# A ninth slot for the expert weights, and SBUF addresses at multiples of 128 bytes

## What is computed

```python
# first block
hx = modulate(rms_norm(x, norm_mix), sh1, sc1)
x = x + g1 * token_mix(hx, ...)           # h @ w_in, gated linear attention, conv, @ w_out
hx2 = modulate(rms_norm(x, norm_ffn), sh2, sc2)
aff = softmax(hx2 @ w_router)             # 512 x 16 experts
gate, idx = top_k(aff.T, 64)              # each expert takes 64 tokens
hid = silu(xs @ w_gate[e]) * (xs @ w_up[e])   # 1024 -> 2048, for 16 experts
x = x + g2 * scatter_add(idx, (hid @ w_down[e]) * gate)
# second block: rmsnorm, w_in, sparse attention, conv branch, merge,
# gated FFN with a convolution, a last gated projection, final rmsnorm
```

## Time and profile before

| | |
|---|---|
| median of 3 executions | 2129.46 us (2128.78 to 2130.61) |
| profiled execution | 2130.91 us, its span 2129.2 us |
| PE matmul busy | 2012.9 us, 95% |
| VectorE, ScalarE busy | 908.8 us (43%), 576.0 us (27%) |
| moved by DMA | 529.58 MB |

### The profile page before, as it was taken

One profiled execution on the slowest core, in us unless ns is written; L12 is line 12 of the kernel. 1 busy time (PEld: TensorE's weight loads), 2 busy tenths in 40 slices (PEclk: granted clock), 3 DMA queues, 4 the chain that ended last, 5 costly groups with the idle time before them and its releaser, 6 DMA issues.

```text
span 2129.2 us, 23757 instructions
## 1 busy us (share of the span) xinstructions
PE 2012.9 (95%) x9886; PEld 1264.0 (59%) x9886; DVE 908.8 (43%) x1489; ACT 576.0 (27%) x899; POOL 58.8 (3%) x107
## 2 busy tenths in 40 slices
PE   6999999899899999988899888999999999999998
PEld 4888777443343424242433323776688888888886
DVE  4666574311021111110101110877897656666545
ACT  5434323100010000000000000527725344344445
POOL 1000000000000000000000000005300000000000
PEclk9999999799999999999999999999999999999999
DMA  9462116699999999999999999151132332323222
GB/s 345 158 229 87 41 41 277 246 384 415 428 428 427 427 428 428 428 428 428 428 428 427 428 428 411 55 141 41 40 119 80 108 100 79 119 79 109 80 98 81
DMA packets 107931, 529.58 MB, mean 249 GB/s; under 512 B 15045, under 2 KB 43825, under 8 KB 82993
## 3 DMA queue, kind: packets, MB, share of 16 engines
q1 hardware_dynamic: 107825, 528.07, 62.0%
HBM read 525.95 MB, written 2.10 MB: 248 GB/s over the span
## 4 chain that ended last, share of the span: by engine, by line
PE 87%; DMA 7%; DVE 3%; issue 2%; ACT 1%; SPq 0%; ACTq 0%; DVEq 0%
PE bank L1033 21%; PE bank L624 14%; PE bank L625 14%; PE bank L626 14%; PE bank L1098 7%; DMA f<-in_w_gate_dram 4%; PE bank L990 3%; PE bank L1007 3%; PE bank L635 2%; DMA f<-in_w_up_dram 1%; PE bank L1197 1%; PE bank L1306 1%; DMA f<-in_w_in_dram 1%; PE bank L836 1%; DMA f<-in_w_ple_gate_dram 0%
## 5 line engine op out<-in xcount | busy, mean ns | idle before, releaser
L1033 PE MATMUL bank<-f,high 128*64 128x512 f32 x2048 | 472.0, 608 | 47.3 <-issue 28.2
L624 PE MATMUL bank<-r 128*128 128x512 f32 (+1 forms) x984 | 389.8, 396 | 4.4 <-DVE r L2037 2.7
L625 PE MATMUL bank<-r 128*128 128x512 f32 (+1 forms) x984 | 385.7, 392 | 0.0
L626 PE MATMUL bank<-r 128*128 128x512 f32 (+1 forms) x984 | 385.4, 392 | 0.0
L1033 PEld LDWEIGHTS bank<-f,high 128*64 128x64 f32 x2048 | 152.1, 139 | 336.4 <-issue 321.8
L1098 PE MATMUL bank<-f,high 128*64 128x512 f32 x1024 | 225.6, 597 | 10.3 <-issue 10.3
L1456 ACT ACTIVATE high<-bank 128x512 f32<-128x512 f32 (+3 forms) x97 | 53.3, 579 | 639.7 <-PE bank L635 303.3
L2371 DVE SCALAR_TENSOR_TENSOR f<-bank,low,f 128x512 f32<-128x512 f32 x64 | 48.1, 751 | 397.1 <-PE bank L1007 396.6
L624 PEld LDWEIGHTS bank<-r 128*128 128x128 f32 (+1 forms) x984 | 184.9, 188 | 51.2 <-issue 5.8
L405 DVE TENSOR_TENSOR r<-f,r 128x1024 fp32r<-128x1024 f32 (+3 forms) x171 | 193.6, 1185 | 36.9 <-ACT r L399 36.8
L626 PEld LDWEIGHTS bank<-r 128*128 128x128 f32 (+1 forms) x984 | 184.6, 188 | 40.4
(11 more groups left out here) (373 smaller groups left out, 1811.7 us busy)
## 6 DMA issues: line engine op xcount, KB each, us to landing
f<-in_w_up_dram SPq DMA_DIRECT2D x64, 2048.0 KB, 21.6
f<-in_w_down_dram SPq DMA_DIRECT2D x64, 2048.0 KB, 21.5
f<-in_w_gate_dram SPq DMA_DIRECT2D x63, 2048.0 KB, 19.8
f<-in_w_in_dram SPq DMA_DIRECT2D x13, 2048.0 KB, 7.9
f<-in_w_up_dram SPq DMA_DIRECT2D x22, 1024.0 KB, 6.5
high<-in_w_ada_dram SPq DMA_DIRECT2D x32, 512.0 KB, 5.6
f<-in_w_ada_dram SPq DMA_DIRECT2D x4, 2048.0 KB, 15.2
f<-in_w_out_dram SPq DMA_DIRECT2D x4, 2048.0 KB, 7.7
```

The costliest lines, as they stand in the source:

```text
L624: pe.matmul(o, wh, xh, start=first, stop=False)
L625: pe.matmul(o, wl, xh, start=False, stop=False)
L626: return pe.matmul(o, wh, xl, start=False, stop=last)
L1033: ins = pe.matmul(o[64 * e:64 * e + 64, :], xsT[p % 2][:, 2 * k + r, 64 * e:64 * e + 64], ws[e](2048 * r + 512 * fc), start=k == 0 and r = ...
```

## The change

The space kept for dynamic DMAs is set to 64 bytes in each partition, and a piece of 16 columns (64 bytes) named `gap` follows it, so that the tensors begin at byte 128. The freed space follows the old end of the layout as a ninth place for expert weights, at M + 28288. The list of turns begins with it: block 0 goes there, block 1 into place 0, and so on. Block 3, not 2, takes `once_x`. Place 7 leaves the list at block 46, not 41, so that eight places are left. The three swaps go. SP issues block 0 ahead of the waits and the two loads of x, and the waits that stood in front of blocks 3, 5 and 9 stand in front of 4, 6 and 10. The small tables move behind XT, so that XT and everything before it is aligned; M becomes 24736, and YH and the places 0, 1 and 4 move by 80 columns to multiples of 128 bytes.

```diff
-            *(f"m{i}" for i in range(8)), "mx", ...
+            *(f"m{i}" for i in range(9)), "mx", ...
-        NW = 53200
-        M = 24832
+        NW = 53024
+        M = 24736
+        ctx.enter_context(nc.sbuf_tensor("gap", [P, 16], F32))
         low, high = lay("low", 0, M, F32), lay("high", M, NW - M, F32)
         ones256 = mem(256)
-        epst = mem(1)
...
-        sel = mem(2)
...
-        mod = v3(mem(3 * 8), 3)
-        small = mem(600)
...
         XT_AT = cursor[0]
         mem(8 * T)
+        small = mem(600)
+        mod = v3(mem(3 * 8), 3)
+        sel, epst = mem(2), mem(1)
-        YH = [memR(512, M + a_) for a_ in (18640, 19152, 19664, 18128)]
+        YH = [memR(512, M + a_) for a_ in (18560, 19072, 19584, 18048)]
-        moe_slot = [own(4096, a_) for a_ in (M + 20176, M + 24272, 0, 4096, M + 16080, 8192, 12288, XT_AT)]
+        moe_slot = [own(4096, a_) for a_ in (M + 20096, M + 24192, 0, 4096, M + 16000, 8192, 12288, XT_AT, M + 28288)]
-        turn_of = list(range(8))
+        turn_of = [8, 0, 1, 2, 3, 4, 5, 6, 7]
-            if n in (2, 7):
+            if n in (3, 7):
                 continue
-            if n == 41:
+            if n == 46:
                 turn_of.remove(7)
-            if n in (49, 55, 61):
-                turn_of[0], turn_of[1] = turn_of[1], turn_of[0]
             load_chunk(N1 - 1)
-            sp.wait_ge(s["pe_inter"], val("pe_inter", 1, 3))
-            ...
-            for i in range(2):
-                sp.dma_start(xres[:, 2 * i:2 * i + 2, :], ...).then_inc(s[f"x{i}"], 16)
             for n in range(NBLK):
+                if n == 1:
+                    sp.wait_ge(s["pe_inter"], val("pe_inter", 1, 3))
+                    ...
+                    for i in range(2):
+                        sp.dma_start(xres[:, 2 * i:2 * i + 2, :], ...).then_inc(s[f"x{i}"], 16)
-                if n == 2:
+                if n == 3:
                     sp.wait_ge(s["v_mix"], val("v_mix", "on", 3))
                     sp.wait_ge(s["pe_mix"], val("pe_mix", "xr", 3, 1))
                     sp.dma_start(once_x, src).then_inc(s["mx"], 16)
...
-                elif n == 9:
+                elif n == 10:
                     sp.wait_ge(s["pe_route"], val("pe_route", "h2", 3, 1))
-                elif n == 3:
+                elif n == 4:
                     sp.wait_ge(s["pe_mix"], val("pe_mix", "res", 3))
-                elif n == 5:
+                elif n == 6:
                     sp.wait_ge(s["pe_mix"], val("pe_mix", "res", 7))
-    nc = _bacc.Bacc("TRN2", target_bir_lowering=False, num_devices=1)
+    nc = _bacc.Bacc("TRN2", target_bir_lowering=False, num_devices=1, dynamic_dma_scratch_size=64)
```

More of the change, by code:

```diff
@@ L20 @@
 DMA_SEMS = (*(f"g{i}" for i in range(6)), *(f"cg{i}" for i in range(4)), *(f"zf{i}" for i in range(4)), "x0", "x1", "rows0", "rows", "small", "ctx", "ada0", "ada1", "ada2", "ada3", "w0", "w1", "ptok", "gf", "out",
-            *(f"m{i}" for i in range(8)), "mx", "my", "mg0", "mg1", "mh0", "mh1", "mq0", "mq1")
+            *(f"m{i}" for i in range(9)), "mx", "my", "mg0", "mg1", "mh0", "mh1", "mq0", "mq1")
 SEMS = (
@@ L489, in sync @@
             load_chunk(N1 - 1)
-            sp.wait_ge(s["pe_inter"], val("pe_inter", 1, 3))
-            sp.wait_ge(s["a_fill"], val("a_fill"))
-            sp.wait_ge(s["v_fill"], val("v_fill"))
-            sp.wait_ge(s["g_y"], val("g_y"))
-            for i in range(2):
-                sp.dma_start(xres[:, 2 * i:2 * i + 2, :], x_v[:, 2 * i:2 * i + 2, :]).then_inc(s[f"x{i}"], 16)
-            for n in range(NBLK):
+            for n in range(NBLK):
+                if n == 1:
+                    sp.wait_ge(s["pe_inter"], val("pe_inter", 1, 3))
+                    sp.wait_ge(s["a_fill"], val("a_fill"))
+                    sp.wait_ge(s["v_fill"], val("v_fill"))
+                    sp.wait_ge(s["g_y"], val("g_y"))
+                    for i in range(2):
+                        sp.dma_start(xres[:, 2 * i:2 * i + 2, :], x_v[:, 2 * i:2 * i + 2, :]).then_inc(s[f"x{i}"], 16)
                 p, r = divmod(n, 24)
```

## The result

The changed kernel takes 2135.28 us (median of 8 executions, 2133.39 to 2138.8), the kernel before 2128.6 (8 executions, 2125.87 to 2130.61): 1.0032 times as long, interval 1.0022 to 1.0043. I had forecast 2121.7 us, faster. It is 6.7 us slower, outside my range. The two profiled executions (2130.91 and 2133.39 us) lie only 2.5 us apart: the one of before is its slowest, the one of after its fastest.

A forecast was written before the change was run, and what follows sets the result against it. Transfers were taken to bound the expert stage from 500 us, after a last pause made by PE, with PE bounding the second block; -4.9 + 1.0 - 3.9 = -7.8 us gave 2121.7 us, range 2119.5 to 2127.0.

The forecast's parts named there:

- Part 1, the ninth place: Expert weight transfers: one block more is loaded before the last queue pause, and this lead becomes 4.9 us less.
- Part 2, x behind block 0: Reload of x before the experts: block 0 delays the second load, PE waits, and everything moves later by 1.0 us.
- Part 3, the addresses: First block's float32r matmuls: operands moved to multiples of 128 bytes all fall to the aligned pace, 3.9 us less.
- were aligned already, so I cost it at nothing: Second block's large matmuls: operands already aligned, so no change; any gain from small tables there stays below 0.2 us.
- The first of my rivals: Slow pace comes from where UL and YH lie relative to the weights; place helps, addresses do not: 2125.6 us, chance 0.17.
- the scan, of which I counted half: GATEC and GATEB matmuls in the first block's scan: 0.86 us from aligned addresses, counted as 0.43 since PE waits for DVE.
- The transfers, at nothing: Expert weight stream: aligned places gain nothing, since 428 GB/s is one rate over all seven places.
- Rival 3: SP's DMA queue needs the reserve taken away, so each block shows its start-up: slower, 470 us at the worst, chance 0.04.

The follow-up runs named there:

- the shifted kernel: Kernel before with a 16-column gap and a 64-byte reserve, so all places shift together and the first tensor begins at byte 256: 2121.49 us, 0.9965.
- the pair with nine places: Changed kernel with M = 24832 and XT 96 columns higher, all operands at one offset: 2113.81 us at base 256; the same 128 bytes higher: 2123.04 us.
- the first experiment: Kernel before with all places shifted together by a 16-column gap and a dynamic DMA reserve of 64 bytes: 2121.49 us, 0.9965.

## Why the prediction was wrong

**What bounds the kernel** was read rightly: transfers from 500 to 1300 us with the last pause made by PE, and a second block that hangs on them with no slack. That is why its matmuls decided.

**Part 1, the ninth place, -4.9.** Right. With part 2 I had -3.9; measured -3.9 and -5.7. That the lead turns into time at 500 us is seen in the long DMA piece that went: with eight places at the new base it is still there (24.48 us from 519.28 on), with nine at the old base it is gone.

**Part 2, x behind block 0, +1.0.** The place was right, the size too high: 0.27 us of wait. The second load landed 2.45 us after PE had begun to turn (I had 2.9), and the first half of the turning took 2.28 us (I had 1.9). The order measured alone gives nothing.

**Part 3, the addresses, -3.9.** Here the prediction failed, in two sentences. "I take the misaligned operand for the cause and let every case fall to the aligned pace" read the rows correctly as to what is slow and wrongly as to why: I took the distance from a multiple of 128 bytes, where the distance between the two operands within 256 counts. The rows could not part the two, since before every aligned operand also stood at distance 0. The sentence that they "were aligned already, so I cost it at nothing" then hid the largest term. M moved by 384 bytes, which leaves a remainder of 128 within 256, and all of the second block went to the slow pace: 14.5 us more. The gain of 3.9 did not come either: UL, UH and YH now stood 128 off the weights, at 0.2334 and 0.233 us. My rule was consistent with the trace and let me skip the question how the change moves `high` against `low`. The first of my rivals named just this, a pace that comes from where UL and YH lie relative to the weights, and I let it only cancel the gain. It works on every matmul, so its other sign was open, and there it was a loss nearly four times the gain that I had counted on.

The 7.8 us that the medians gained ahead of the second block are the very sum that I had forecast, by luck: 3.9 of my 7.8 were to come from addresses that gave nothing, and faster transfers that I had at nothing stood in for them.

Where the distance is really made 0 for UL and YH, they do get the pace that I forecast, and the time gets 1.9 to 2.0 us, half of the 3.9 that I summed. What takes the rest isn't shown; the scan, of which I counted half, is one candidate, and these executions differ among themselves by as much (2122.38 to 2128.98 for that run).

**The transfers, at nothing.** Also wrong, to the good: "428 GB/s is one rate over all seven" was true of places 64 bytes apart, and said nothing of the base under them. With the base at a multiple of 256 bytes the stream runs at 430. From 4.893 to 4.863 us a block, over 168 blocks behind the last pause, is 5 us; the medians say 7.4 to 9.2. That the last of the 16 signals of block 191 also trails the first by less (6.5 us in the shifted kernel, 7.8 before; 5.9 and 6.7 in the pair with nine places) is about 1 us more. The loads at the start are faster too, which I had overlooked: from 20 to 30 us the rate is 387 to 393 GB/s in the four kernels at the old base and 408 or 409 at the new one, and the shifted kernel starts its first expert matmul at 407.6 us, where before has 410.2. What these leave of the 7.4 to 9.2 us is within the scatter; why the base matters is open.

**Rival 3**, that the queue needs the reserve, fell with the first experiment: 64 bytes of it, and a faster stream.

**Lines and ports.** The Trainium skill (page "SBUF — State Buffer", section "Specifications (TRN2)") has lines of 16 bytes with a cost for crossing to a new one. Distances of 64 and 128 bytes are whole lines, and the runs show 2.2 and 5.6 ns a matmul all the same. The Trainium skill, on the same page (section "Who interferes with whom"), gives TensorE two read ports, one for the moving operand and one for loading weights, independent of each other. The runs agree in so far as the plain float32 matmuls of the experts keep 216 ns at every distance tried; that the pace of the float32r ones follows the distance between the two operands does not fit with it, and here the measurement decides.

## What to carry to other kernels

A new layout changes distances between operands also where nothing seems to move. When tensors are laid out by hand, compare the offset of each operand with that of its partner, not with a round number: in these kernels a distance of 0 within 256 bytes is worth 2.5% of a float32r matmul's time against a distance of 128. And a rule that fits all rows of a trace, where two properties always occur together in it, must be priced with both, because the change may part them.

The version with nine places, M = 24832 and the base at 256 beats both kernels: 2113.81 and 2114.84 us in two measurements, 0.7% below before and 1.0% below the change. The single edit of M by 32 columns gets 2115.73.

## What the runs showed of the hardware

- Float32r matmuls of 512 columns, back to back at granted clock 1.00: 0.2267 us at distance 0 or 256 between stationary and moving operand, 0.2289 at 64 with the input moving and 0.2333 with it stationary, 0.2323 to 0.2334 with both parts of the input at 128. At distance 0, shifting both by 128 bytes changes nothing; at 128 it changed 0.2323 to 0.2333. The moving YH took 0.2333 in the kernel before, where it stood 64 off and YL did not; why that is more than 0.2289 is open, and so is the mechanism.
- Plain float32 matmuls of the experts: 128 of them over down blocks 16 to 23 (line 1097 in the changed kernel) take 27.62 us in every kernel, so no difference at any of these.
- 2 MB blocks into SBUF: 4.863 to 4.865 us each (430 GB/s) in six kernels whose first tensor begins at a multiple of 256 bytes, with the upper places at 0, 64 or 128 past one (4.868 in the run with M = 24784); 4.893 to 4.894 (428 GB/s) in the four whose base is 128 past one, whatever the places above. Where the places stand at two offsets, blocks at multiples of 256 come 4.84 us behind the one before and the others 4.89, with the same mean. The cause is open.
